# Gelu, weights and diagonals of the expert stage made on ScalarE two slots at a time instead of four

## What is computed

```python
def expert_chunk(args):
    xc, idc, gc = args
    u = jnp.take(u_tab, idc, axis=0)
    a = jax.nn.gelu(jnp.einsum('cd,chkd->chk', xc, u), approximate=False)
    vv = jnp.take(v_tab, idc, axis=0)
    return jnp.einsum('chk,chkd->cd', gc * a, vv)
```

## Time and profile before

| | |
|---|---|
| median of three runs | 1786.49 us |
| the profiled execution | 1784.41 us |
| its span, first to last instruction | 1782.7 us |
| PE busy | 1290.3 us (72%) |
| DVE busy | 1111.1 us (62%) |
| POOL busy | 1018.7 us (57%) |
| ACT busy | 514.7 us (29%) |
| moved by DMA | 623.57 MB, mean 350 GB/s |

### The profile page before, as it was taken

One profiled execution on the slowest core, in us unless ns is written; L12 is line 12 of the kernel. 1 busy time (PEld: TensorE's weight loads), 2 busy tenths in 40 slices (PEclk: granted clock), 3 DMA queues, 4 the chain that ended last, 5 costly groups with the idle time before them and its releaser, 6 DMA issues.

```text
span 1782.7 us, 15641 instructions
## 1 busy us (share of the span) xinstructions
PE 1290.3 (72%) x4541; PEld 717.6 (40%) x4568; DVE 1111.1 (62%) x2405; ACT 514.7 (29%) x1398; POOL 1018.7 (57%) x1061
## 2 busy tenths in 40 slices
PE   8987675676774887877865698977877467666654
PEld 6555342342431545533342264634444134222221
DVE  3356777638487547645467848755549758755455
ACT  3322234313222312343222332354222212322221
POOL 2026666645566454665656655566656656666664
PEclk9999887888887999978988799988988788777776
DMA  9349999998999899998998999998998989999997
GB/s 356 107 165 360 364 388 376 359 345 323 394 399 368 298 347 354 407 383 304 418 412 307 355 372 412 409 384 317 364 418 332 358 312 341 339 372 374 351 353 296
DMA packets 186333, 623.57 MB, mean 350 GB/s; under 512 B 25600, under 2 KB 25600, under 8 KB 186256
## 3 DMA queue, kind: packets, MB, share of 16 engines
q0 software_dynamic: 147456, 536.94, 78.8%
q1 hardware_dynamic: 38800, 85.71, 12.9%
HBM read 621.53 MB, written 1.05 MB: 349 GB/s over the span
## 4 chain that ended last, share of the span: by engine, by line
PE 36%; DVE 23%; issue 18%; another core or an unknown queue 9%; DMA 7%; POOL 3%; ACT 3%; SPq 0%; DVEq 0%; ACTq 0%; PEldq 0%; POOLq 0%
PE acc L1650 19%; DVE u_ring L840 11%; PE pair L1503 4%; PE pair L1575 4%; DVE h L850 4%; PE pair L1490 3%; DMA u_ring<-in_peer_u,ids 3%; POOL v_ring L553 2%; POOL u_ring L539 2%; DMA wbuf<-in_fox_w_q 1%; DVE scratch L704 1%; DMA wbuf<-in_peer_w_q 1%; PE pair L1532 1%; ACT L1221 1%
## 5 line engine op out<-in xcount | busy, mean ns | idle before, releaser
L1650 PE MATMUL acc<-v_ring,diag 128*128 128x512 f32 x1524 | 801.4, 684 | 387.7 <-issue 186.0
L553 POOL DMA_INDIRECT v_ring<-in_peer_v,ids x512 | 507.3, 991 | 477.9 <-PE acc L1650 283.2
L840 DVE SCALAR_TENSOR_TENSOR u_ring<-u_ring,pair 128x1024 f32<-128x1024 f32 x508 | 599.6, 1217 | 212.6 <-DMA u_ring<-in_peer_u,ids 175.2
L1650 PEld LDWEIGHTS acc<-v_ring,diag 128*128 128x128 f32 x1524 | 327.5, 222 | 810.5 <-issue 749.9
L539 POOL DMA_INDIRECT u_ring<-in_peer_u,ids x512 | 498.4, 973 | 270.3 <-issue 246.4
L1221 ACT ACTIVATE gelus<-dots 128x4 f32<-128x4 f32 x128 | 26.4, 207 | 653.1 <-DVE u_ring L840 431.5
L850 DVE SCALAR_TENSOR_TENSOR h<-v_ring,weights_s,h 128x1024 f32<-128x1024 f32 x128 | 164.4, 1284 | 19.0 <-issue 7.0
L1575 PE MATMUL pair<-xT,wbuf 128*128 128x128 f32 x896 | 112.1, 281 | 30.1 <-issue 15.2
L1234 ACT ACTIVATE diag<-ident,weights_s 128x128 f32<-128x128 f32 x381 | 125.5, 391 | 10.9 <-issue 4.2
L1575 PEld LDWEIGHTS pair<-xT,wbuf 128*128 128x128 f32 x896 | 107.4, 196 | 34.5 <-issue 20.3
L1221 ACT ACT_TABLE_LOAD x56 | 71.8, 1283 | 169.6 <-DVE u_ring L840 150.8
(11 more groups left out here) (199 smaller groups left out, 1042.0 us busy)
## 6 DMA issues: line engine op xcount, KB each, us to landing
wbuf<-in_peer_w_q SPq DMA_DIRECT2D x24, 1024.0 KB
wbuf<-in_kv_w SPq DMA_DIRECT2D x10, 1024.0 KB
u_ring<-in_peer_u,ids POOLq DMA_INDIRECT x512
v_ring<-in_peer_v,ids POOLq DMA_INDIRECT x512
wbuf<-in_fox_w_q SPq DMA_DIRECT2D x8, 1024.0 KB
wbuf<-in_fox_w_o SPq DMA_DIRECT2D x8, 1024.0 KB
wbuf<-in_gla_w_o SPq DMA_DIRECT2D x7, 1024.0 KB
wbuf<-in_gla_w_in SPq DMA_DIRECT2D x6, 1024.0 KB
```

The costliest lines, as they stand in the source:

```text
L553: pool.indirect_dma_start(v_ring[:, j, :], None, v_rows, bass.IndirectOffsetOnAxis(ap=ids[:, b, at:at + 1], axis=0)).then_inc(v_loaded[j], 16)
L840: nc.vector.scalar_tensor_tensor(out=u_ring[:, j, :], in0=u_ring[:, j, :], scalar=1.0, in1=near, op0=ALU.mult, op1=ALU.mult, accum_out=dot ...
L1650: ins = nc.tensor.matmul(acc[:, i, :], diag[:, k, :], v_ring[:, j, i * HALF:(i + 1) * HALF], start=False, stop=False)
```

## The change

A new constant `TWO` is 2, and `TWOS = RING // TWO` is 4. ScalarE works each half in two pairs of slots. For a pair it waits for two dots, makes Gelu of two columns, makes two weights, and then makes the diagonals of the pair. `dots_free` and `gelu_ready` count pairs, so they rise four times in a round and no longer twice. VectorE waits for `dots_free` ahead of dots 0, 2, 4 and 6. After dot 4 it waits for the second pair's `gelu_ready` (`r * TWOS + 2`). ScalarE's wait for `vec_free` moves to the start of the first half.

```diff
             def half(ph, r, q):
 
                 layer, b = PHASES[ph]
-                s = slice(q * SUB, (q + 1) * SUB)
-                act.wait_ge(u_free, r * RING + (RING + (q + 1) * SUB))
-                nc.scalar.activation(gelus[:, s], dots[:, s], ACT.Gelu).then_inc(dots_free, 1)
-                act.wait_ge(dots_free, r * (RING // SUB) + (RING // SUB + q + 1))
                 if q == 0:
                     act.wait_ge(vec_free, r * VEC + VEC)
-                for j in range(q * SUB, (q + 1) * SUB):
-                    ins = nc.scalar.activation(
-                        weights_s[:, j:j + 1], gelus[:, j:j + 1], ACT.Copy,
-                        scale=gates[:, b, bass.ds(r * RING + (j - ph * SLOTS), 1)])
-                ins.then_inc(gelu_ready, 1)
-                act.wait_ge(gelu_ready, r * (RING // SUB) + (q + 1))
-                for k, j in enumerate(PE_SLOTS):
-                    if j // SUB == q and not is_last(r, j):
-                        act.wait_ge(v_free, r * len(PE_SLOTS) + (k + 1))
-                        nc.scalar.activation(diag[:, k, :], ident[:, :], ACT.Copy,
-                                             scale=weights_s[:, j:j + 1]).then_inc(diag_ready, 1)
+                for t in range(q * SUB // TWO, (q + 1) * SUB // TWO):
+                    slots = range(t * TWO, (t + 1) * TWO)
+                    s = slice(t * TWO, (t + 1) * TWO)
+                    act.wait_ge(u_free, r * RING + (RING + (t + 1) * TWO))
+                    nc.scalar.activation(gelus[:, s], dots[:, s], ACT.Gelu).then_inc(dots_free, 1)
+                    act.wait_ge(dots_free, r * TWOS + (TWOS + t + 1))
+                    for j in slots:
+                        ins = nc.scalar.activation(
+                            weights_s[:, j:j + 1], gelus[:, j:j + 1], ACT.Copy,
+                            scale=gates[:, b, bass.ds(r * RING + (j - ph * SLOTS), 1)])
+                    ins.then_inc(gelu_ready, 1)
+                    act.wait_ge(gelu_ready, r * TWOS + (t + 1))
+                    for k, j in enumerate(PE_SLOTS):
+                        if j in slots and not is_last(r, j):
+                            act.wait_ge(v_free, r * len(PE_SLOTS) + (k + 1))
+                            nc.scalar.activation(diag[:, k, :], ident[:, :], ACT.Copy,
+                                                 scale=weights_s[:, j:j + 1]).then_inc(diag_ready, 1)
```

On VectorE:

```diff
-                dve.wait_ge(dots_free, r * (RING // SUB) + (q + 1))
                 for j in range(q * SUB, (q + 1) * SUB):
+                    if j % TWO == 0:
+                        dve.wait_ge(dots_free, r * TWOS + (j // TWO + 1))
                     dve.wait_ge(u_loaded[j], r * 16 + 16)
...
-                    dve.wait_ge(gelu_ready, r * (RING // SUB) + 1)
+                    dve.wait_ge(gelu_ready, r * TWOS + TWOS // 2)
```

More of the change, by code:

```diff
@@ L31 @@
 SUB = 4
+TWO = 2
+TWOS = RING // TWO
 ROUNDS = SLOTS // RING
@@ L1101, in _ @@
             experts(3, HALVES - 2, HALVES)
-            dve.wait_ge(gelu_ready, len(PHASES) * HALVES)
+            dve.wait_ge(gelu_ready, len(PHASES) * ROUNDS * TWOS)
             dve.wait_ge(vec_free, (len(PHASES) * ROUNDS + 1) * VEC)
@@ L1244, in take_k @@
                     qkT[:, b, 1, :, :].rearrange("p h t -> p (h t)"), pair_of(("k", b))[:, 0, :], ACT.Copy))
-            act.sem_inc(dots_free, RING // SUB)
+            act.sem_inc(dots_free, TWOS)
             act.wait_ge(consts, 3)
```

## The result

The changed kernel takes 1779.89 us (median of 14 runs, 1767.87 to 1797.19), the kernel before 1791.31 us (14 runs, 1782.61 to 1803.14). The ratio is 0.9913, 95% interval 0.989 to 0.9936: 0.87% faster, 15.6 us. It is taken over the fast executions; the two medians by themselves are 11.4 us apart. The forecast was 43.5 us, 1743 us in all. Its wide range (1706 to 1786 us) held the time and the narrow one (1716 to 1772 us) did not; the gain was off by a factor of nearly three. The experiments show that the forecast's size comes out on some chips (0.9731, 44 us) and not on others, and where the gain stays behind there.

A forecast was written before the change was run, and what follows sets the result against it. A loop between DVE, ACT and PE was taken as the bound. 42.6 us (16 bursts x 2.66) plus 3.9 capped minus 3 for POOL gave 43.5 us, so 1743 us; range 1716 to 1772, wide range 1706 to 1786.

The forecast's parts named there:

- The 2.66 us: First diagonal of a half: comes earlier by two dots (2.28 us) and two weights (0.38 us), together 2.66 us.
- The count of bursts: PE's expert matmul bursts on the chain: 20, of which 16 gain 2.66 us, three 1.3 us, one nothing.
- The whole burst, and the matmuls queued behind it, move by the 2.66 us.: PE: two slots last 3.5 us, the second pair follows within 2.28 us, so everything queued moves 2.66 us earlier.
- a sign of being wrong: Rounds near 300 us: if they keep their 23.2 us instead of 20.6, the prediction is wrong.
- The loop read from the earlier trace: Round near 320 us: loop DVE, ACT, PE, DVE takes 23.23 us, with 3.3 us to give before POOL's 19.9.
- the 29 waits of PE on "issue": PE before expert bursts: 186.0 us idle in 29 waits, read as waits for a half's first diagonal.
- ACT's price: ScalarE: 128 more Gelus, 24 us by the skill page, hidden by idle time; costed at nothing, at most 59 us.
- The waits on DVE: VectorE: four dots_free waits a round and the second pair's weights cost -0.2 to +0.46 us a round, taken as zero.
- the gain is taken back: POOL's 1.24 us an issue or an unlanded gather replaces the diagonal; some 5 us remain, 1781 us; chance 0.14.
- ACT becomes late: ScalarE: extra Gelus cost table loads or register work, a pair takes over 2.28 us; 1808 us; chance 0.07.
- open at full clock: PE bursts: shorter idle keeps the clock up, 16 bursts gain another 2.6 us each; 1701 us; chance 0.08.
- get slower: PE bursts starting on two slots stay longer at half clock, 15 us over 20 bursts; 1801 us; chance 0.05.

The follow-up runs named there:

- s_second: Against the kernel before, slots 0 to 3 made together, then 4 and 5, then 6 and 7: 0.9854 and 0.9956 on late chips, 0.9705 on a prompt one.
- s_first: Against the kernel before, slots 0 and 1, then 2 and 3, then 4 to 7 together: 1.0076 on a late chip, 1.0003 on a prompt one.
- a_two: The changed kernel, unchanged, run again on a second late chip, against the kernel before: 0.9898.
- s_first_two: Slots 0 and 1, then 2 and 3, then 4 to 7 together, run again on a prompt chip, against the kernel before: 1.0003.
- c_pairs_v5: The changed kernel with VectorE's two v rows moved from behind dot 4 to behind dot 5, on a prompt chip, against the kernel before: 0.9684.
- a_three: The changed kernel, unchanged, on a prompt chip, against the kernel before: 1601.32 us beside 1645.15 us, 0.9731.

## Why the forecast was right or wrong

*The 2.66 us.* Right: 2.65 us measured.

*The count of bursts.* On prompt chips the product of count and shift came out: the delay of 2.3 us cost as much as 21 bursts, and the change brought 43.8 us for a forecast of 43.5. As a list it was partly wrong. The rounds of the bursts at 283, 306, 330 and 352 us gain nothing together without late signals, and 16 rounds gain 2.1 to 6.2 us each, not 2.66; the largest is that of the listed burst at 877 us. The agreement to 0.3 us is luck. That an earlier first diagonal of the second half makes the kernel faster is not: on prompt chips s_second has the whole gain and s_first none.

*"The whole burst, and the matmuls queued behind it, move by the 2.66 us."* This is the step that failed, on the chips for which the forecast was made. The burst moves. What waits for it, POOL for slots of v and DVE for the level, is let go by a signal that there comes up to 8 us after PE's records end, at a time that the burst alone doesn't set. In the profiled result the five rounds from 252 us on still take 23 us on average, as the forecast had named for a sign of being wrong, but unevenly: one has no pause at all and takes 20.7 us, and in the next POOL waits 6 us and it takes 26.9. POOL's 477.9 us of idle became 479.4 there, and 453.9 in a_two. So by the two ratios 16 to 18 us of 43 were kept. That the late signals took the rest is inferred from these rows and from the difference between the chips.

*The loop read from the earlier trace rows.* The 7.21 us that DVE waited were read as PE's lateness. The release was "remote", with PE's records over 1.6 us earlier, and a prompt chip runs this round in 20.74 us. I gave such waits nothing in the last 230 us, and overlooked that the earlier trace rows has 9% of the chain on "another core or an unknown queue". Reading the 29 waits of PE on "issue" as waits for a diagonal was right.

*ACT's price.* Right for Gelu. Gelu went from 26.4 to 51.2 us, 24.8 more. The rule on ScalarE's fixed part (Trainium skill, "ScalarE: Activation LUTs", section "What ACT_TABLE_LOAD costs") gave 24, and the trace agrees. But ACT's busy time grew by 40.8 us (514.7 to 555.5): the weights and diagonals, made two at a time, took 22 us more in all (109.1 to 123.7 and 125.5 to 132.9), which the forecast left out. All of it stays hidden behind 549.2 us of idle. *The waits on DVE.* I took zero with at most 0.46 us a round; in the round at 1029 us it was 0.96 us, and the waits for these weights are 20.0 us in all. On prompt chips s_first_two shows that it costs nothing measurable.

*The rivals.* On late chips the result has the size of "the gain is taken back" (1781), not its mechanism: neither POOL's 1.24 us nor a gather ended the waits. On prompt chips that rival is the next bound, as the waits of c_pairs_v5 suggest. "ACT becomes late" named register work; it exists on late chips (below) in the last rounds only. The bursts did not open at full clock (8.59 and 8.85 us in a_three), and they did not get slower either.

*Open.* What makes a signal late, and why some chips have them and others not. Nothing here tells whether it is the chip or something else that uses it, or whether the signal or a slow step of an engine's sequencer is the late part.

## What to carry to other kernels

Before a shift of one engine's work is priced, look at how the waits behind it end, and measure the time from the producer's end to the waiter's start. Where it is 0.05 to 0.15 us the release was prompt, even under the mark "issue". Where it is several us, as under "remote" here, the release follows something else, and a burst that ends earlier passes on only a part: here about 40%. Measure on more than one chip if there is a choice, as the same edit was worth 1% and 2.7%. And a delay of known length put into the kernel before is a second estimate of how many bursts lie on the path, beside the chain of waits.

## What the hardware showed that I had not expected

*Chips differ by 9%.* The same kernel takes 1645 and 1786 to 1798 us, with issues of 0.94 us, dots of 1.22 us and gathers at the same peak (418 to 420 GB/s in the best slices) on both.

*Late signals.* On late chips signals come up to 9 us after the records' end, several at once, from TensorE (7.9 us at 304 us) and from VectorE to itself (8.88 us). The changed kernel's POOL waits there hold a row that no prompt chip has:

```profile
POOL v_ring L555 <- remote: 54.8, 21, 3.9
```

*Slow steps between ScalarE's instructions.* In the last stage, a hardware loop, ACT of the changed kernel on the late chip, and below it a_three in the same stage on a prompt one:

```profile
1662.46 0.20 ACT L1228 ACTIVATE gelus<-dots 128x2 f32<-128x2 f32 x1 [2.13 <-issue]
...
1666.07 0.40 ACT L1239 ACTIVATE diag<-ident,weights_s 128x128 f32<-128x128 f32 x1 [2.50 <-issue]
...
1671.67 0.29 ACT L1231 ACTIVATE weights_s<-gelus,gates 128x1 f32<-128x1 f32 x1 [2.62 <-issue]
1673.06 0.29 ACT L1231 ACTIVATE weights_s<-gelus,gates 128x1 f32<-128x1 f32 x1 [1.10 <-issue]
```

```profile
1505.03 0.20 ACT L1228 ACTIVATE gelus<-dots 128x2 f32<-128x2 f32 x1 [9.15 <-DVE u_ring L843]
1505.37 0.48 ACT L1231 ACTIVATE weights_s<-gelus,gates 128x1 f32<-128x1 f32 x2
1505.96 0.69 ACT L1239 ACTIVATE diag<-ident,weights_s 128x128 f32<-128x128 f32 x2
```

From Gelu to the first diagonal it takes 3.61 us there and 0.93 us here. A part of that can be a late signal, since the diagonal waits for `v_free`. But between the two weights of a pair the kernel has no wait at all, only the place of the gate to work out from the loop's register, and there ACT stands 1.10 us where on the prompt chip the two weights run on without a pause (0.48 us for both). Such stretches lie in the last 230 us. Whether slow steps and late signals have one cause isn't shown; that a slow sequencer is behind both is a rival that no run tests.
